# Two-block transformer step on one core: gate sums, turns, output norm and evictions moved in a hand-written order

## The chip, the cores and the metric

The kernel runs on one core of a Trainium2 chip, in one launch. The metric is device microseconds (us) of that core; lower is better. The engines are named as the profile names them: PE is TensorE, DVE is VectorE, ACT is ScalarE, POOL is GpSimd, SP is SyncE, which here only issues DMAs.

## The reference, cut to what matters

Two blocks follow each other on 256 latent tokens with 256 context tokens of width 1024, all in float32. The first block has two layers: a mixer out of a gated delta net and a chunked gated MLP, and multi-head latent attention (MLA); each has a gated feed-forward part with a depthwise convolution. The second block has dilated and sparse attention pairs (DIL, DSA), then cross attention (CRS) and an MLP. The change is mostly in the first mixer:

```python
def chunk_gmlp(u, v, ln_g, ln_b, ws, bs):                 # the "spatial" half, y_a
    u = gelu(u); v = layer_norm(gelu(v), ln_g, ln_b)
    s = einsum('gij,bnjgd->bnigd', ws, chunks(v)) + bs
    return u * s

def gdn_chunked(q, k, v, g, beta, s0):                    # the delta rule, y_b
    gcum = cumsum(g); decay = exp(tril(gcum_i - gcum_j))
    a_mat = strict_tril((k*beta) k^T * decay)
    t_mat = inverse(eye + a_mat)                          # built here in levels
    u = t_mat (v*beta);  w = t_mat (k*beta*exp(gcum))
    attn = q k^T * decay;  kdec = k * exp(gcum_end - gcum)
    scan over chunks: v_new = u - w s; o = (q*exp(gcum)) s + attn v_new
                      s = s * exp(gcum_end) + kdec^T v_new

def ab_mixer(...):
    a_u, a_v, qkv, gate, alpha, beta = split(h @ w_in)
    y_b = rms_norm(o_forward + o_backward, norm_g) * silu(gate)
    y = concatenate([y_a, y_b]) @ w_out                   # chunks 0-3 y_a, 4-7 y_b
```

Context tokens are scanned first (st=0), then the latent ones (st=1), which start from the context's final states.

## The kernel before, in words

**Projections.** Every weight is float32 and goes through the PE as a high and a low part in the rounded type fp32r. SP streams blocks of 512 KB into a ring of four slots. ACT's `split` (L1577) makes `w_high`, DVE's `low` (L2089) makes `w_low`, and `mm3` (L646 to L648) multiplies three times for each of the 8 chunks of 128: high by high, high by the low part of the activation, low by high. A tile is 128 output columns by up to 512 tokens, so 24 matmuls; tiles alternate between two banks, and ACT or DVE evicts each. For `low(t + 2)` to run, `split(t + 2)` must be done, and that waits for a PE tile that frees the slot.

**Order.** There is no planner. Each engine has its own hand-written instruction list, joined by semaphores, and each engine works strictly in the order of its list. Any instruction that waits holds everything that is behind it on its engine.

**The input projection, `in0`.** 25 tiles. The gates are tile 12 and are summed over tokens on the way: PE turns the gates and sums them (L792, L793) behind tile 16, out of `g_tok`, a copy by DVE (L2263). DVE makes cumulative sums and their combinations (L2265 to L2277), ACT takes one Exp of all of them (L1730), DVE multiplies two by beta (L2281, L2282; semaphore `g_fac`). Behind tile 18 PE spreads rows of these for the first quarter (L760, L761), and behind 20, 22 and 23 for the others (`ROWS_AT`). DVE also does `mod_tile(t)` in each tile (L2220, two products of 128x1024 for the modulation of a later layer), whose rows SP loads between the weight blocks.

**The levels.** 28 steps, 7 levels for 4 quarters, build the inverse. In each, PE multiplies (L893, L900), POOL masks (`lev_ct`, L1483), ACT evicts (`lev_m`, L1789), PE multiplies (L917, L920), DVE adds (L2385, L2386; in the first level L2359, L2380). Between the steps stand other jobs, given by the step number k: turns of the keys (L814, `TURNS`), spatial turns (L829), the layer norm of the spatial half on ACT, DVE and POOL (L1757, L1760, L2313 to L2321, L1507).

**The scan and `out0`.** Behind the scan of the latents come the output norm (ACT squares L1768, PE `out_sums` L850, ACT root L1772, DVE reciprocal L2333, PE `out_spread` L857, DVE L2341 and a product with the gate), then the split of y in high and low, then tiles 0 and 1 of `out0`, whose chunks 0 to 3 take y_a and 4 to 7 take y_b. The low parts of y_a are four DVE subtractions (L2432).

**Attention.** In `attend` (MLA, CRS) and `pair_step` (DIL, DSA) ACT takes the Exp of one step (L1941, L1960) and evicts the turned probabilities of the step before last, `probs_t` (L1947, L1967). PE turns probabilities (L1144, L1170) and multiplies by values (L1198, L1225, L1293). DVE does the maxima before the Exp and the divisions behind it.

## Time and profile before

| | us |
|---|---|
| median of 3 runs | 1676.14 |
| lowest, highest | 1676.03, 1677.31 |
| profiled execution, its own time | 1686.6 |
| its span, first to last instruction | 1684.8 |
| PE busy in it | 1568.6 (93%) |
| DVE, ACT, POOL busy | 1136.8, 797.0, 120.1 |
| mean granted PE clock | 0.965 |

Stages in the trace, us from the start of the span: `in0` ends about 219, levels of the context to about 278, scan of the latents to 391, `out0` from 398, MLA attention 922 to 972, DIL pairs 1309 to 1366, DSA pairs 1371 to 1402, CRS 1451 to 1469.

In a timeline row the first number is the start, the second the duration. A bracket at the end holds how long the engine had idled and which instruction released it. "x8" groups eight instructions, and the duration is that of the group from first start to last end.

### The profile page before, as it was taken

The page shows a single profiled execution, that of the slowest core. Times are in us where ns is not written, and L with a number is a line of the kernel's source. Part 1 is how long each engine was busy: PE and PEld are TensorE (multiplying, and loading weights), DVE is VectorE, ACT ScalarE, POOL GpSimd, SP SyncE. Part 2 cuts the span into 40 slices and gives each one's busy share as a digit, 9 for nine tenths or more (in the row PEclk, how much of TensorE's full clock was granted, in tenths as well). Part 3 has the DMA queues.
Part 4 walks back from the last instruction along what each step waited for, and adds up shares of the span by engine and source line. Part 5 has one row for each costly group of instructions (what it writes and reads, how often), then busy time and mean ns, then how long its engine had stood idle before and what let it go on. Part 6 is the DMA issues. An engine that isn't in the chain of part 4 may idle for free.

```text
span 1684.8 us, 30970 instructions
## 1 busy us (share of the span) xinstructions
PE 1568.6 (93%) x11414; PEld 1379.8 (82%) x11414; DVE 1136.8 (67%) x1902; ACT 797.0 (47%) x1436; POOL 120.1 (7%) x134
## 2 busy tenths in 40 slices
PE   5899978789999999999899999999999889999998
PEld 3687768788677777788787599999898668999998
DVE  5975765654599999966545458885565665477644
ACT  2553545142454444422255457775444445566532
POOL 2000032420100000000000010001000001010000
PEclk8999989999899999999899999999899999999999
DMA  9344420001155555555333035556443223255552
GB/s 356 118 176 161 150 77 3 2 3 38 63 188 186 187 182 179 182 180 174 122 125 100 2 101 187 187 187 214 160 163 126 88 75 104 98 188 184 178 195 91
DMA packets 62955, 230.77 MB, mean 137 GB/s; under 512 B 6800, under 2 KB 8080, under 8 KB 62352
## 3 DMA queue, kind: packets, MB, share of 16 engines
q1 hardware_dynamic: 61408, 223.37, 39.2%
q0 software_dynamic: 1168, 5.80, 1.0%
q8 instruction: 64, 1.05, 0.3%
q10 hardware_dynamic: 288, 0.33, 0.1%
q14 instruction: 27, 0.22, 0.0%
HBM read 228.43 MB, written 1.05 MB: 136 GB/s over the span
## 4 chain that ended last, share of the span: by engine, by line
PE 80%; DVE 11%; ACT 5%; issue 3%; POOL 1%; DMA 1%; DVEq 0%; ACTq 0%; POOLq 0%
PE proj L646 21%; PE proj L648 21%; PE proj L647 21%; DVE w_low L2089 2%; PE bank L698 1%; ACT w_high L1577 1%; PE bank L900 1%; PE bank L1198 1%; PE bank L917 1%; PE bank L920 1%; PE proj L1102 1%; PE proj L1103 1%; PE proj L1104 1%; DMA ident_sb<-ident 1%; DVE h_low L2122 1%
## 5 line engine op out<-in xcount | busy, mean ns | idle before, releaser
L646 PE MATMUL proj<-h_high,w_high 128*128 128x256 f32 (+1 forms) x1768 | 585.0, 331 | 22.3 <-DVE h_low L2122 13.7
L648 PE MATMUL proj<-h_high,w_low 128*128 128x256 f32 (+1 forms) x1768 | 571.6, 323 | 0.0
L647 PE MATMUL proj<-h_low,w_high 128*128 128x256 f32 (+1 forms) x1768 | 571.5, 323 | 0.0
L2089 DVE TENSOR_TENSOR w_low<-w_raw,w_high 128x1024 fp32r<-128x1024 f32 x322 | 393.3, 1224 | 191.0 <-ACT w_high L1577 189.6
L1577 ACT ACTIVATE w_high<-w_raw 128x1024 fp32r<-128x1024 f32 x322 | 338.5, 1056 | 243.8 <-PE proj L648 240.7
L646 PEld LDWEIGHTS proj<-h_high,w_high 128*128 128x128 f32 x1768 | 337.0, 191 | 65.0 <-issue 18.3
L648 PEld LDWEIGHTS proj<-h_high,w_low 128*128 128x128 f32 x1768 | 337.6, 191 | 27.6
L647 PEld LDWEIGHTS proj<-h_low,w_high 128*128 128x128 f32 x1768 | 337.1, 191 | 25.2
L648 PE MATMUL proj<-act_high,w_low 128*128 128x256 f32 (+1 forms) x608 | 189.9, 312 | 0.0
L646 PE MATMUL proj<-act_high,w_high 128*128 128x256 f32 (+1 forms) x608 | 189.5, 312 | 0.4 <-DVE w_low L2089 0.4
L647 PE MATMUL proj<-act_low,w_high 128*128 128x256 f32 (+1 forms) x608 | 189.5, 312 | 0.0
L646 PEld LDWEIGHTS proj<-act_high,w_high 128*128 128x128 f32 x608 | 114.1, 188 | 8.1 <-DVE w_low L2089 0.8
L647 PEld LDWEIGHTS proj<-act_low,w_high 128*128 128x128 f32 x608 | 113.8, 187 | 7.7
L648 PEld LDWEIGHTS proj<-act_high,w_low 128*128 128x128 f32 x608 | 114.3, 188 | 6.6
L1656 ACT ACTIVATE conv_in<-proj 128x512 f32<-128x512 f32 (+1 forms) x100 | 49.9, 499 | 120.3 <-PE proj L648 117.2
L2220 DVE SCALAR_TENSOR_TENSOR mod_products<-a_ring,cond_rows 128x1024 f32<-128x1024 f32 x80 | 103.6, 1295 | 0.1
L1450 POOL TENSOR_TENSOR tmp<-tmp 128x256 f32<-128x256 f32 (+1 forms) x40 | 43.7, 1099 | 797.5 <-ACT tmp L1593 619.0
L2220 DVE SCALAR_TENSOR_TENSOR a_ring<-a_ring,cond_rows 128x1024 f32<-128x1024 f32 x80 | 97.6, 1220 | 0.0
L2171 DVE SCALAR_TENSOR_TENSOR conv_mid<-conv_in,cols_sb,conv_mid 128x512 f32<-128x512 f32 (+1 forms) x100 | 63.5, 635 | 14.0 <-DVE conv_mid L2169 8.2
L2169 DVE SCALAR_TENSOR_TENSOR conv_mid<-conv_in,cols_sb,conv_mid 128x512 f32<-128x512 f32 (+1 forms) x100 | 63.3, 633 | 12.4 <-ACT conv_mid L1657 10.5
L1657 ACT ACTIVATE conv_mid<-proj,cols_sb 128x512 f32<-128x512 f32 (+1 forms) x100 | 58.9, 589 | 0.0
L2185 DVE SCALAR_TENSOR_TENSOR x<-proj,mod,x 128x256 f32 (+1 forms) x48 | 21.7, 480 | 48.1 <-PE proj L648 48.1
(406 smaller groups left out, 1917.7 us busy)
## 6 DMA issues: line engine op xcount, KB each, us to landing
w_raw<-w_stream SPq DMA_DIRECT2D x322, 512.0 KB, 3.3
a_ring<-a_stream SPq DMA_DIRECT2D x80, 512.0 KB, 3.2
a_first<-a_head SPq DMA_DIRECT2D x4, 1024.0 KB, 18.0
a_first<-a_stream SPq DMA_DIRECT2D x4, 1024.0 KB, 18.6
x<-x_in SPq DMA_DIRECT2D x1, 2048.0 KB, 10.4
late_tab<-late_tables POOLq DMA_DIRECT2D x1, 1408.0 KB, 6.5
cond_rows<-cond_rows SPq DMA_DIRECT2D x1, 1024.0 KB, 5.7
cond_rows<-cond_rows POOLq DMA_DIRECT2D x1, 1024.0 KB, 5.1
```

Source lines behind the costliest of these rows:

```text
L646: mm(out_, wh, xh, start=first, stop=False)
L647: mm(out_, wh, xl, start=False, stop=False)
L648: return mm(out_, wl, xh, start=False, stop=last)
L1450: nc.gpsimd.tensor_tensor(squares(name, 0), squares(name, 0), squares(name, k), ALU.add).then_inc(n_early, 1)
L1577: f(wh(n), RAW[:, n % 4, :], ACT.Copy).then_inc(w_high, 1)
L1656: f(XP[:, k % 2, 0:n, 1:SEQ + 1], PL[t % 2][:, 0:width].rearrange("p (s t) -> p s t", s=n), ACT.Copy)
L1657: f(C1[:, k % 2, 0:width], PL[t % 2][:, 0:width], ACT.Identity, scale=C[:, ds(taps + 3 * k + 1 + 3 * per * it, 1)]).then_inc(tile_out, 1)
L2089: v.tensor_tensor(wl(n), RAW[:, n % 4, :], wh(n), ALU.subtract).then_inc(w_low, 1)
L2169: v.scalar_tensor_tensor(o, XP[:, k % 2, 0:n, 0:SEQ], C[:, ds(taps + 3 * k + 3 * per * it, 1)], o, ALU.mult, ALU.add).then_inc(conv_mid, 1)
L2171: v.scalar_tensor_tensor(o, XP[:, k % 2, 0:n, 2:SEQ + 2], C[:, ds(taps + 3 * k + 2 + 3 * per * it, 1)], o, ALU.mult, ALU.add).then_inc(con ...
L2185: last = v.scalar_tensor_tensor(o, y, g, o, ALU.mult, ALU.add)
L2220: v.scalar_tensor_tensor(o, w, 1.0, cond[:, s, :], ALU.mult, ALU.mult, accum_out=MODF[:, ds(2 * (A_FIRST + j) + s + 2 * off, 1)]).then_inc ...
```

## The change

**A. `in0`.** DVE copies `g_tok` ahead of `low(18)` instead of behind it. The block of cumulative sums goes from tile 17 to the end of tile 16, the two products with beta from behind `low(20)` to ahead of it. ACT's Exp of the sums goes ahead of `split(19)`, with its wait. `mod_tile` gets ahead by one from tile 19 on, so that tile 23 has none. The closing of the modulation (L2096, L2102) and `low(26)` go into the levels, steps 3 and 6.

**B. Levels of the context.** The second turn of the keys is at step 8 instead of 6; the spatial turns, their evictions and each step of the layer norm are two or three steps later. POOL clears its 128x2048 table in two halves.

**C. Output.** The low parts of y_a are made on POOL. PE does tile 0's chunks 0 to 3 of `out0` ahead of `out_sums`, two chunks of tile 1 ahead of `out_spread` and two behind it, then the chunks of y_b for the context tokens, then for the latents. The products with the gate and the splits of the latents are in two halves.

**D. Evictions.** In `attend` and `pair_step` ACT evicts `probs_t` ahead of the Exp instead of behind it.

**E. `out2`.** 18 matmuls of tile 1 stand ahead of the last `dsa_out`.

```diff
-        TURNS = [(3, 6), (16, 20)]
+        TURNS = [(3, 8), (16, 20)]
 # PE, spatial_gate
-                if k in (9, 11):
+                if k in (12, 14):
 # PE, behind the scan
+            both = slice(0, T2)
+            weights(B0["out0"])
+            free_bank(T0["out0"])
+            pe.wait_ge(G["y_a"], 4)
+            out_part(0, range(4), both)
             out_sums(1)
+            weights(B0["out0"] + 1)
+            free_bank(T0["out0"] + 1)
+            out_part(1, range(2), both)
             out_spread(1)
-            first_tiles("out0", slice(0, T2), T2, lambda k: (G["y_a"], 4) if k < 4 else (G["y_b"], 2),
-                        [(j, k) for ks in (range(4), range(4, KC)) for j in range(2) for k in ks])
+            out_part(1, range(2, 4), both)
+            pe.wait_ge(G["y_b"], 1)
+            for j in range(2):
+                out_part(j, range(4, KC), CTX)
+            pe.wait_ge(G["y_b"], 2)
+            for j in range(2):
+                out_part(j, range(4, 6), LAT)
+            pe.wait_ge(G["y_b"], 3)
+            for j in range(2):
+                out_part(j, range(6, KC), LAT, KC - 1).then_inc(pe_done, 1)
 # PE, out2
+            out2_products(0)
             dsa_out(3)
-            project("out2", LAT, SEQ, lambda k: (A["at_y"], DSA.e0 + 2))
+            out2_products(1)
 # POOL, behind the levels of the latents
+            for d in range(2):
+                pool.wait_ge(sc_s[d], 3)
+            for t in range(4):
+                tok = slice(t * P, (t + 1) * P)
+                pool.wait_ge(G["sp_hi"], t + 1)
+                nc.gpsimd.tensor_tensor(HL[:, 0:4, tok], UV[:, 0:4, tok], HH[:, 0:4, tok], ALU.subtract).then_inc(G["y_a"], 1)
 # ACT, in0
             for t in range(GATES, 25):
+                if t == 17:
+                    act.wait_ge(G["g_cum"], 1)
+                    f(EX[:], EX[:], ACT.Exp).then_inc(G["g_exp"], 1)
                 if t < 24:
                     split(t + 2)
...
-                if t == 17:
-                    act.wait_ge(G["g_cum"], 1)
-                    f(EX[:], EX[:], ACT.Exp).then_inc(G["g_exp"], 1)
 # ACT, layer norm in the levels
-                if k in (10, 12):
+                if k in (13, 15):
-                if k in (14, 15):
+                if k in (17, 18):
-                if k == 16:
+                if k == 18:
                     act.wait_ge(G["ln_sq"], 4)
                     f(SM[:, 58:62], SM[:, 58:62], ACT.Sqrt, scale=1.0 / 512, bias=col("eps")).then_inc(G["ln_std"], 1)
-                if 18 <= k < 22:
+                if 20 <= k < 24:
 # ACT, attend (pair_step likewise)
+                    if 2 <= a < ly.n + 2:
+                        p = a - 2
...
+                        f(PT[:, p % 2, 0:ly.kt, :], ..., ACT.Copy).then_inc(A["at_pt"], 1)
                     if a < ly.n:
                         r = a % 3
                         act.wait_ge(A["at_m"], ly.a0 + a + 1)
...
-                    if 2 <= a < ly.n + 2:
-                        p = a - 2
...
 # DVE, in0
             for t in range(GATES, 24):
+                if t == 16:
+                    dve.wait_ge(G["g_tr"], 1)
+                    v.tensor_copy(GTOK[:], ...).then_inc(G["g_tok"], 1)
+                if t == 18:
+                    dve.wait_ge(G["g_exp"], 1)
+                    v.tensor_tensor(BE, BE, beta, ALU.mult)
+                    v.tensor_tensor(BR, BR, beta, ALU.mult).then_inc(G["g_fac"], 1)
                 low(t + 2)
...
+                if t in ROWS_AT:
+                    decays(0, ROWS_AT[t])
+                    triangles(0, ROWS_AT[t])
+                for j in ((t,) if t < 19 else (19, 20) if t == 19 else (t + 1,) if t < 23 else ()):
+                    mod_tile(j, CB0, PROD0)
...
+            def last_modulations(k):
+                if k == 3:
+                    dve.wait_ge(m_acc, 2 + 2 * MOD_IN)
+                    link(modulation(A_FIRST, MOD_IN))
+                    gains(0, 1).then_inc(mod_ready, 1)
+                if k == 6:
+                    low(26)
 # DVE, output norm
-                dve.wait_ge(G["on_n"], 2 * st + 2)
-                v.tensor_tensor(QKV[:, 8:12, x], QKV[:, 8:12, x], GATE[:, :, x], ALU.mult).then_inc(G["on_y"], 1)
+                for p in range(2):
+                    o = QKV[:, 8 + 2 * p:10 + 2 * p, x]
+                    dve.wait_ge(G["on_n"], 2 * st + p + 1)
+                    v.tensor_tensor(o, o, GATE[:, 2 * p:2 * p + 2, x], ALU.mult).then_inc(G["on_y"], 1)
```

DVE in `in0`, from tile 16 to tile 18. `w_low` is `low`, `g_cum` to `factors` the block of sums, and the `mod_products` and `a_ring` pair is one `mod_tile`. Before:

```order
106 L2089 TENSOR_TENSOR w_low<-w_raw,w_high 128x1024
107 L2268 TENSOR_SCALAR qk_log_factors<-qk_lengths 128x4x4
...
115 L2277 TENSOR_TENSOR factors<-qk_log_factors 128x32
116 L2220 SCALAR_TENSOR_TENSOR mod_products_100,mod<-a_ring,cond_rows_99 128x1024
117 L2220 SCALAR_TENSOR_TENSOR a_ring,mod<-a_ring,cond_rows_99 128x1024
118 L2089 TENSOR_TENSOR w_low<-w_raw,w_high 128x1024
119 L2281 TENSOR_TENSOR factors<-factors,g_tok 128x32
120 L2282 TENSOR_TENSOR factors<-factors,g_tok 128x32
```

The same place after:

```order
105 L2269 SCALAR_TENSOR_TENSOR a_ring,mod<-a_ring,cond_rows_99 128x1024
106 L2328 TENSOR_SCALAR qk_log_factors<-qk_lengths 128x4x4
...
114 L2337 TENSOR_TENSOR factors<-qk_log_factors 128x32
115 L2138 TENSOR_TENSOR w_low<-w_raw,w_high 128x1024
116 L2269 SCALAR_TENSOR_TENSOR mod_products_100,mod<-a_ring,cond_rows_99 128x1024
117 L2269 SCALAR_TENSOR_TENSOR a_ring,mod<-a_ring,cond_rows_99 128x1024
118 L2310 TENSOR_TENSOR factors<-factors,g_tok 128x32
119 L2311 TENSOR_TENSOR factors<-factors,g_tok 128x32
120 L2138 TENSOR_TENSOR w_low<-w_raw,w_high 128x1024
```

The sums have gone ahead of the `w_low` of tile 17, and the products with beta ahead of that of tile 18.

DVE where `in0` ends and the levels begin; `inv_u_halves` and `inv_t` are the first level's quarters. Before:

```order
154 L2248 TENSOR_TENSOR a_halves<-bank,decay 64x256 x2
155 L2251 TENSOR_TENSOR a_cross<-bank,decay 64x256
156 L2220 SCALAR_TENSOR_TENSOR mod_products_100,mod<-a_ring,cond_rows_99 128x1024
157 L2220 SCALAR_TENSOR_TENSOR a_ring,mod<-a_ring,cond_rows_99 128x1024
158 L2096 TENSOR_TENSOR mod<-mod,cols_sb 128x48
159 L2102 SCALAR_TENSOR_TENSOR gains<-mod,cols_sb 128x16
160 L2089 TENSOR_TENSOR w_low<-w_raw,w_high 128x1024
161 L2359 TENSOR_TENSOR inv_u_halves<-gdn_tab,lev_ct 128x256 x2
```

After:

```order
156 L2297 TENSOR_TENSOR a_halves<-bank,decay 64x256 x2
157 L2300 TENSOR_TENSOR a_cross<-bank,decay 64x256
158 L2414 TENSOR_TENSOR inv_u_halves<-gdn_tab,lev_ct 128x256 x2
159 L2435 TENSOR_TENSOR inv_t<-gdn_tab,bank 128x256 x2
160 L2414 TENSOR_TENSOR inv_u_halves<-gdn_tab,lev_ct 128x256
161 L2435 TENSOR_TENSOR inv_t<-gdn_tab,bank 128x256
162 L2414 TENSOR_TENSOR inv_u_halves<-gdn_tab,lev_ct 128x256
163 L2435 TENSOR_TENSOR inv_t<-gdn_tab,bank 128x256
164 L2145 TENSOR_TENSOR mod<-mod,cols_sb 128x48
```

The first level's products stand right behind `a_cross`; nothing of the modulation or of the next weight is between them.

PE where the scan of the latents ends and `out0` begins. Before:

```order
930 L970 MATMUL bank<-qkv,state 128x128 x4
931 L984 MATMUL bank<-attn_t,v_new 128x128 x8
932 L850 MATMUL bank<-ones,out_squares 128x1 x8
933 L857 MATMUL bank<-ident_sb,small 128x128 x8
934 L646 MATMUL proj<-h_high,w_high 128x512
935 L647 MATMUL proj<-h_low,w_high 128x512
```

After:

```order
931 L984 MATMUL bank<-attn_t,v_new 128x128 x8
932 L646 MATMUL proj<-h_high,w_high 128x512
...
943 L648 MATMUL proj<-h_high,w_low 128x512
944 L850 MATMUL bank<-ones,out_squares 128x1 x8
945 L646 MATMUL proj<-h_high,w_high 128x512
...
950 L648 MATMUL proj<-h_high,w_low 128x512
951 L857 MATMUL bank<-ident_sb,small 128x128 x8
952 L646 MATMUL proj<-h_high,w_high 128x512
```

Twelve matmuls of tile 0 now stand ahead of the sums of squares, and six of tile 1 between these and the spreading of the roots.

## Rows read from the trace of the kernel before

**Rows 1.** The page: busy us, share of the span and instructions of each engine.
```profile
PE 1568.6 (93%) x11414; PEld 1379.8 (82%) x11414; DVE 1136.8 (67%) x1902; ACT 797.0 (47%) x1436; POOL 120.1 (7%) x134
```

**Rows 2.** Waits of PE, 150 to 282 us: total, times, longest.
```profile
PE bank L893 <- POOL lev_ct L1483: 4.3, 1, 4.3
...
PE proj L814 <- DVE k_decay L2302: 2.6, 1, 2.6
PE proj L829 <- DVE k_decay L2302: 2.6, 1, 2.6
```

**Rows 3.** Timeline of PE around the gate sums and the first spread rows.
```profile
155.66 0.40 PE L648 MATMUL proj<-h_high,w_low 128*128 128x512 f32 x1
158.75 0.40 PE L792 MATMUL bank<-g_tok,gdn_tab 128*128 128x16 f32 x2 [2.70 <-DVE g_tok L2263]
...
160.09 0.77 PE L646 MATMUL proj<-h_high,w_high 128*128 128x512 f32 x1
...
173.48 0.39 PE L647 MATMUL proj<-h_low,w_high 128*128 128x512 f32 x1
173.71 0.40 PE L648 MATMUL proj<-h_high,w_low 128*128 128x512 f32 x1
176.77 0.80 PE L760 MATMUL bank<-ident_sb,log_rows 128*128 128x128 f32 x2 [2.67 <-DVE factors L2282]
...
179.96 0.48 PE L646 MATMUL proj<-h_high,w_high 128*128 128x512 f32 x1
```

**Rows 4.** Windows: us, busy (count) of PE, PEld, DVE, ACT, POOL; clock, DMA.
```profile
160.00:166.00 6.00, 6.00 (x16) 4.74 (x16) 0.99 (x2) 0.00 (x0) 0.00 (x0) 0.50 0.49 175
...
176.00:180.00 4.00, 3.23 (x17) 3.23 (x17) 0.71 (x3) 2.44 (x3) 0.00 (x0) 0.57 0.63 237
...
225.00:231.00 6.00, 6.00 (x88) 5.55 (x86) 1.96 (x4) 1.36 (x6) 2.95 (x5) 0.51 0.40 146
...
244.00:248.00 4.00, 4.00 (x69) 3.80 (x69) 0.44 (x2) 1.54 (x5) 0.73 (x1) 0.57 0.02 4
...
391.00:399.00 8.00, 5.91 (x35) 5.73 (x36) 3.26 (x7) 1.33 (x2) 0.00 (x0) 0.79 0.01 2
```

**Rows 5.** Timeline of DVE at tile 16.
```profile
157.24 1.23 DVE L2089 TENSOR_TENSOR w_low<-w_raw,w_high 128x1024 fp32r<-128x1024 f32 x1 [2.56 <-ACT w_high L1577]
158.38 0.32 DVE L2263 COPY g_tok<-bank 128x160 f32<-128x160 f32 x1
```

**Rows 6.** Timeline of DVE at the start of the levels.
```profile
218.88 1.74 DVE L2220 SCALAR_TENSOR_TENSOR mod_products<-a_ring,cond_rows 128x1024 f32<-128x1024 f32 x1
...
223.28 0.75 DVE L2359 TENSOR_TENSOR inv_u_halves<-gdn_tab,lev_ct 128x256 f32<-128x256 f32 x2
```

**Rows 7.** Timeline of ACT in the layer norm: table load and root.
```profile
259.66 1.28 ACT L1760 ACT_TABLE_LOAD   x1
260.96 0.30 ACT L1760 ACTIVATE small<-small,cols_sb 128x4 f32<-128x4 f32 x1
```

**Rows 8.** Timeline of PE behind the scan of the latents.
```profile
392.50 1.95 PE L850 MATMUL bank<-ones,out_squares 128*128 128x1 f32 x16 [1.93 <-ACT out_squares L1768]
395.04 3.52 PE L857 MATMUL bank<-ident_sb,small 128*128 128x128 f32 x16 [0.60 <-DVE small L2333]
```

**Rows 9.** Timeline of POOL in the layer norm.
```profile
266.11 1.28 POOL L1507 TENSOR_TENSOR uv<-uv,ln_rows_sb 128x512 f32<-128x512 f32 x1 [0.69 <-DVE uv L2321]
```

**Rows 10.** Timelines of ACT and of PE in MLA.
```profile
934.61 0.59 ACT L1947 ACTIVATE probs_t<-bank 128x512 f32<-128x512 f32 x1
...
934.54 0.66 PE L1144 MATMUL bank<-ident_sb,probs 128*128 128x128 f32 x4
935.25 1.16 PE L1198 MATMUL bank<-probs_t,mla_v 128*128 128x128 f32 x8
```

**Rows 11.** Waits of PE on evicted probabilities, in DIL and in DSA.
```profile
PE bank L1225 <- ACT probs_t L1967: 1.7, 3, 0.6
PE bank L1293 <- ACT probs_t L1967: 2.2, 4, 0.7
```

More of the change, by code:

```diff
@@ L819, in spatial_gate @@
             def spatial_gate(k):
-                if k in (9, 11):
-                    for t in (k - 9, k - 8):
+                if k in (12, 14):
+                    for t in (k - 12, k - 11):
                         if t >= 2:
@@ L985, in _, with out_part @@
                         last.then_inc(sc_o[d], 1)
+            def out_part(j, chunks, x, final=None):
+                n, t = B0["out0"] + j, T0["out0"] + j
+                for k in chunks:
+                    w = slice(k * P, (k + 1) * P)
+                    last = mm3(PL[t % 2][:, x], wh(n)[:, w], wl(n)[:, w], HH[:, k, x], HL[:, k, x], k == 0, k == final)
+                return last
+            both = slice(0, T2)
[3 more added lines that the diff above has]
+            out_part(0, range(4), both)
             out_sums(1)
+            weights(B0["out0"] + 1)
+            free_bank(T0["out0"] + 1)
+            out_part(1, range(2), both)
             out_spread(1)
-            first_tiles("out0", slice(0, T2), T2, lambda k: (G["y_a"], 4) if k < 4 else (G["y_b"], 2),
-                        [(j, k) for ks in (range(4), range(4, KC)) for j in range(2) for k in ks])
+            out_part(1, range(2, 4), both)
[8 more added lines that the diff above has]
+                out_part(j, range(6, KC), LAT, KC - 1).then_inc(pe_done, 1)
             for s in (2, 3):
@@ L1307, in _, with out2_products @@
                     dsa_out((a - 6) // 2)
-            dsa_out(3)
-            project("out2", LAT, SEQ, lambda k: (A["at_y"], DSA.e0 + 2))
+            out2_order = [(1, k) for k in (4, 5, 6, 7, 0, 2)], [(0, k) for k in (4, 5, 6, 7, 0, 2, 1, 3)] + [(1, 1), (1, 3)]
+            def out2_products(part):
+                n, t = B0["out2"], T0["out2"]
+                for i, (j, k) in enumerate(out2_order[part]):
+                    if i == 0:
+                        weights(n + j)
+                        free_bank(t + j)
+                        pe.wait_ge(A["at_y"], DSA.e0 + 1 + part)
+                    w = slice(k * P, (k + 1) * P)
+                    last = mm3(PL[(t + j) % 2][:, 0:SEQ], wh(n + j)[:, w], wl(n + j)[:, w], HH[:, k, LAT], HL[:, k, LAT], k == 4, k == 3)
+                    if k == 3:
+                        last.then_inc(pe_done, 1)
+            out2_products(0)
+            dsa_out(3)
+            out2_products(1)
+            for s in (2, 3):
+                tile(B0["out2"] + s, T0["out2"] + s, LAT, SEQ)
+            with pe.Fori(1, 2) as i:
+                for s in range(4):
+                    tile(B0["out2"] + s, T0["out2"] + s, LAT, SEQ, 4 * i)
             project("xq", CTX, SEQ, h_ready("cross"), beside="cross")
@@ L1953, in pair_step @@
             def pair_step(ly, a, out_bank, out_chunk):
+                if 2 <= a < ly.n + 2:
+                    p = a - 2
+                    nk = 1 + p % 2
+                    act.wait_ge(A["at_t"], ly.a0 + p + 1)
+                    act.wait_ge(A["at_o"], ly.a0 + p - 1)
+                    f(PT[:, p % 2, 0:2 * nk, :], BK[2 + p % 2][:, 0:2 * nk * P].rearrange("p (k q) -> p k q", k=2 * nk), ACT.Copy).then_inc(A["at_pt"], 1)
                 if a < ly.n:
@@ L2277, in _ @@
                     v.tensor_tensor(BR, by_k, by_q, ALU.subtract).then_inc(G["g_cum"], 1)
-                if t == 18:
-                    beta = GTOK[:, :, 32:40].rearrange("p t (d h) -> p t d h", d=2)
-                    dve.wait_ge(G["g_exp"], 1)
-                    v.tensor_tensor(BE, BE, beta, ALU.mult)
-                    v.tensor_tensor(BR, BR, beta, ALU.mult).then_inc(G["g_fac"], 1)
-                    dve.wait_ge(gdn_in, 16)
-                if t in ROWS_AT:
-                    decays(0, ROWS_AT[t])
-                    triangles(0, ROWS_AT[t])
-                mod_tile(t, CB0, PROD0)
-            dve.wait_ge(m_acc, 2 + 2 * MOD_IN)
-            link(modulation(A_FIRST, MOD_IN))
-            gains(0, 1).then_inc(mod_ready, 1)
-            low(26)
+            def last_modulations(k):
+                if k == 3:
+                    dve.wait_ge(m_acc, 2 + 2 * MOD_IN)
[3 more added lines that the diff above has]
+                    low(26)
             def keys(st, k):
@@ L2427, in _ @@
                         ins.then_inc(sc_out[d], 1)
+            dve.wait_ge(G["on_hi"], 1)
+            v.tensor_tensor(HL[:, 4:8, CTX], QKV[:, 8:12, CTX], HH[:, 4:8, CTX], ALU.subtract).then_inc(G["y_b"], 1)
             out_factor(1)
[L2429 to L2432 removed]
             out_norm(1)
[L2434 to L2436 removed]
+            for p in range(2):
+                dve.wait_ge(G["on_hi"], 2 + p)
+                v.tensor_tensor(HL[:, 4 + 2 * p:6 + 2 * p, LAT], QKV[:, 8 + 2 * p:10 + 2 * p, LAT], HH[:, 4 + 2 * p:6 + 2 * p, LAT], ALU.subtract).then_inc(G["y_b"], 1)
             def project(name, width=None, gate=None, loops=2):
```

57 lines of the change are left out of this document (24 added, 33 removed).

## The prediction, as it was put on record before the changed kernel ran

> **What bounds the kernel now.** I read the page first: PE is busy for 93% of the span, DVE for 67%, ACT for 47% [rows 1]. The change removes no matmul, so it can gain only where PE stands idle, and where PE runs at half its clock. Next I read PE's waits by stage. In the 130 us around the end of `in0` and the levels there are a few long ones: 4.3 us on POOL's mask, and two of 2.6 us on DVE's `k_decay` [rows 2]; two of 2.7 us stand at the gate sums [rows 3]. Third, the windows: behind each of these waits the granted clock is 0.50 to 0.57 for some us, though PE is busy all through [rows 4]. So such a wait costs twice: its own time, and the lost clock behind it (a granted 0.50 is 1.2 GHz, 1.00 is 2.4 GHz). Last I read what DVE and ACT do just before PE is released.
>
> The sum is made against the profiled execution (1686.6 us), which is 10.5 us above the median of 1676.14. These savings are microseconds of waits, so I take them off the median unscaled.
>
> **Part A, gate sums, -10.5 us.** Tile 16 of PE ends at 155.7+0.4, and DVE copies `g_tok` at 158.38 only because `low(18)` stands before it, and waits 2.56 us for ACT and then takes 1.23 [rows 5]. The copy needs nothing of ACT's. Moved ahead, it is done before PE gets there: PE's 2.70 goes. From the last product of tile 16 to tile 17 are 4.43 us (155.66 to 160.09); one product pace of 0.23 and the four small products at full clock, about 0.9, remain, so 3.3 are saved. Then the clock: from 160 to 166 it was 0.50 [rows 4], so that from the first to the last product of tiles 17 and 18, 160.09 to 173.71, it took 13.6 us; 47 products, 0.23 apart as at 173.48 and 173.71 [rows 3], are 10.7: 2.9 saved. The second wait, 2.67 at 176.77, ends with `factors` L2282 [rows 3]: this now stands ahead of `low(20)`, and the sums ahead of `low(19)`. By durations of before, the sums are done at about 161.8, the Exp at 162.4, the two products at 167.4 behind `low(19)` and `mod_tile`, and tile 18 ends at 167.8: in time by 0.4. From 173.71 to 179.96 are 6.25 us, of which one product's pace and the sixteen small ones at full clock (0.11 each, as the levels' pace of 0.106 shows) need 1.9: 4.3 saved. 3.3 + 2.9 + 4.3 = 10.5.
> What is late next? ACT's Exp now holds `split(19)`. That one is released by the end of tile 17, at 162.3, so it is late by some 0.1 us, and its cover is tile 18 (5.5 us) before its high part is needed. `mod_tile` one ahead: DVE may wait 0.2 to 0.5 us for a row that SP loads; the cover is the same tile. If the clock does not recover, only the two waits go: -5.4, the small end. There is no large end beyond 10.5, since PE then runs with no gap.
>
> **Part B, start of the levels and turns, -12.2 us.** PE waits 4.3 us for the first level's masks, since POOL waits for DVE. DVE comes to the first level's products at 223.28, after 4.4 us of modulation, gains and `low(26)` that begin at 218.88 [rows 6]. These now stand in steps 3 and 6. The wait of 4.3 [rows 2] goes, and with it the six us at 0.51, which are 2.9 of lost clock (6 x 0.49) [rows 4]; 0.5 stays, for the masks of POOL which each follow PE's product by a short wait. 4.3 + 2.9 - 0.5 = 6.7. Behind that, the key turn's 2.6 goes: a step of the levels is about 1.4 us, so step 8 instead of 6 gives DVE 2.8 us more to make `k_decay`. Of the spatial turn's 2.6 I leave 1.2, since it is three steps later, but the key turn ahead of it has moved by two and `low(26)` (1.22 us) is now in between: 1.4 saved, and 1.5 of the four us at 0.57 [rows 2, 4]. 6.7 + 2.6 + 1.4 + 1.5 = 12.2. The layer norm keeps its length: each job moves by two or three steps. The root now falls in the same step as the last squares, so its table load may hold an eviction of the levels by 1.3; the next steps, which have nothing else on ACT, give it back. Small end: only the first 4.3 and the key turn, -6.9. Large end -14, if the spatial wait goes altogether.
> The row for the table load shows 1.28 us, and the root starts 0.02 us behind its end [rows 7]; ACT's eviction before it had ended at the load's start. The Trainium skill, page "ScalarE: Activation LUTs", section "What ACT_TABLE_LOAD costs", gives about 1283 ns and a drain of about 1380 ns for each switch. The load agrees; the drain is not in this trace. By the page the root in step 18 would cost an estimated 1.4 us more, and part B would be 10.8.
>
> **Part C, output, -4.2 us.** PE idled 1.93 for ACT's squares and 0.60 for the root, and the 16 spread products took 3.52 us [rows 8] where 1.8 is full clock: the window shows 0.79 [rows 4]. Now twelve products (2.7 us) fill the first wait and six (1.4) the second; 1.93 + 0.60 + 1.7 = 4.2. They need the low parts of y_a before about 390.4, where the scan ends. POOL makes four of 128x512; a POOL product of that size took 1.28 [rows 9], so 5.1 us, from about 384.1, when the third state is out: done at 389.2. Bound: 1.76 each, as POOL's sums of squares go (L1450), ends at 391.1, and PE waits 0.7. The four DVE subtractions that went away hid behind the spread and gain nothing by themselves. Small end -2.5, large end -5.
>
> **Part D, evictions first, -6.1 us.** In MLA the turn that began at 934.54 is four products and over by 935.0, but the values' products behind it began at 935.25, when the eviction of 934.61, which stood behind an Exp, had ended (935.20) [rows 10]. That is 0.2 in a period of 6.2 us, which repeats some seven times: -1.5. In DIL the wait on `probs_t` is 1.7 in three places [rows 11]; it goes, and one copy's length more, 0.6 to 0.7, comes off the wait for the divisions behind it: -2.4. In DSA the four waits sum to 2.2 [rows 11], all on the copy that stood behind two Exps: -2.2. The cost is an Exp that starts one copy later, 0.59; it is hidden while the Exp waits for DVE's maximum. Ends: -3 if the waits just go over to the divisions, -9 if the clock too is held in DIL.
>
> **Part E, `out2`, 0.** Eighteen half-width products of 0.12 us are 2.1 us, moved ahead of the last `dsa_out`; PE then waits for the same split of the last chunk. From -1.5 to +0.7.
>
> Sum: -10.5 - 12.2 - 4.2 - 6.1 = -33.0. One us back for new short dips of the clock: -32, so 1676.1 - 32 = 1644.1.
>
> **The rivals.** *R1, the waits move within the levels.* DVE and ACT have the same work in fewer us, and the turns, which wait for DVE's products, come as late as before against the start of the levels. For it: both turns wait for the same DVE line [rows 2]. Against it: the moves are 2.8 and 4.2 us of steps against waits of 2.6. Then B gives only 4: -24, 1652. *R2, the clock stays low.* The waits go, but the granted clock falls elsewhere in these stages, since many waits of 0.3 to 0.7 remain. It costs back 2.9 + 1.6 (A), 2.9 + 1.5 (B) and 1.7 (C), together 10.6, less the 1 allowed: -22.4, 1654. *R3, more than the sum.* The large ends of B, C and D: -42, 1634. *R4, slower.* One mechanism: evicting first puts the Exp behind a copy that waits for PE's turns, and the new wait of ACT before `split(19)` does the same in `in0`; PE gets more short waits in place of a few long ones, and is granted half the clock over long stretches. For it: two stages got more waits of ACT on PE. Place: levels, scan and attention, where most windows show 0.95 to 1.00. Half the clock costs one us for each us of products, so it turns slower when more than 33 us of PE's work go at 0.5 that now go at 1.0; for 50 us it gives +17, 1693. Against it: the low stretches of these stages all stand behind waits of 1.9 us or more [rows 2, 3, 8]. *R5, nothing moves.* If the new gate wait on ACT held as long as the old ones on DVE, A is nothing; all parts would have to fail: 1676. The order of instructions shows each move, so this is small.
>
> **How the numbers follow.** Forecast (-26 to -39) 0.70; R1 0.12; R2 0.08; R3 0.05; R4 0.02; R5 0.03. The small ends together (5.4 + 6.9 + 2.5 + 3 - 0.7) are -17.1, or 1659; the large ends, taken as not all coming together, -40, or 1636. The range 1636 to 1658 holds the forecast, R1 and R2 and most of the unknown costs, and leaves out R3 to R5. A measurement of this kernel can tell 0.2%, 3.4 us, from no change. Faster 0.95, same 0.03, slower 0.02.
>
> **What would show it.** Right: no idle of PE before `g_tok` and `factors`, clock near 1.00 from 155 to 180; the first level starts within 1 us of the end of `in0`; PE goes from the scan into `out0` with no gap; waits on `probs_t` gone in DSA. Wrong: PE waits at the spread of tile 18 on `factors` (A's margin is 0.4 us), at the turns on `k_decay`, at L893 on POOL, at tile 0 of `out0` on POOL's subtraction; or the same waits gone, but windows at 0.5 beside them.

## The result, and the profile after

| | before | after |
|---|---|---|
| median of 5 runs, us | 1676.6 | 1652.93 |
| lowest, highest | 1676.03, 1679.1 | 1649.54, 1654.63 |
| ratio, 95% interval | | 0.9846 [0.9831, 0.986] |
| profiled execution, its span | 1684.8 | 1647.8 |
| mean granted PE clock in it | 0.965 | 0.977 |

The medians differ by 23.7 us; the two traced executions by 37.0. A second measurement of both kernels (below) gave 0.9818 [0.9795, 0.984], -30.6 us. Both intervals lie wholly below 1, so the changed kernel is faster, by 1.5 to 1.8%. The forecast was -32. Some microseconds stand between these numbers, and they are the subject of the first experiment.

The page of the changed kernel, engines and granted clock:

```profile
PE 1546.7 (94%) x11438; PEld 1364.2 (83%) x11438; DVE 1133.9 (69%) x1901; ACT 796.8 (48%) x1437; POOL 124.6 (8%) x139
...
PEclk9999999999899999999899999999899999999999
```

PE has 22 us less busy time than in [rows 1], though it does the same products: what went there is PE at half its clock. (Against a second trace of the kernel before, below, it is 13 us.) The matmul count differs by missing records and by the split tiles.

**Gate sums.** The timeline of ACT and that of DVE, changed kernel, around tiles 17 and 18:

```profile
161.00 0.31 ACT L1766 ACTIVATE factors<-factors 128x128 f32<-128x128 f32 x1 [2.94 <-DVE factors L2337]
161.63 1.06 ACT L1625 ACTIVATE w_high<-w_raw 128x1024 fp32r<-128x1024 f32 x1 [0.32 <-PE proj L648]
```

```profile
166.26 0.19 DVE L2311 TENSOR_TENSOR factors<-factors,g_tok 128x32 f32<-128x32 f32 x1
```

ACT's Exp is over at 161.31 and `split(19)` still idles 0.32 us for PE behind it, so the new wait ahead of it costs nothing. The second product with beta ends at 166.45; PE uses it at 166.87, a margin of 0.4 us. PE shows no idle time where [rows 3] had 2.70 and 2.67. The windows of the changed kernel (us, busy and count of PE, PEld, DVE, ACT, POOL, clock, DMA) show the full clock through `in0` and the levels, where [rows 4] had 0.50, 0.57 and 0.51:

```profile
155.00:165.00 10.00, 10.00 (x49) 8.38 (x48) 6.86 (x16) 6.08 (x7) 0.00 (x0) 1.00 0.58 208
165.00:175.00 10.00, 10.00 (x53) 8.51 (x52) 7.38 (x19) 4.53 (x6) 1.29 (x1) 1.00 0.29 106
...
207.00:213.00 6.00, 4.84 (x106) 4.02 (x106) 5.59 (x12) 2.01 (x4) 4.45 (x7) 1.00 0.01 3
```

**Levels.** PE's waits, 200 to 262 us, changed kernel:

```profile
PE bank L917 <- ACT lev_m L1837: 3.9, 3, 1.8
PE proj L829 <- DVE k_decay L2355: 1.2, 1, 1.2
...
PE bank L893 <- POOL lev_ct L1523: 0.5, 1, 0.5
```

Against [rows 2] the first masks cost 0.5 in place of 4.3, the key turn nothing in place of 2.6, the spatial turn 1.2 in place of 2.6. The waits on ACT's evictions grew: L917 from 2.6 in four to 3.9 in three, and L924 from 0.6 in two to 1.2 in three.

**Output.** The timeline of PE behind the scan, changed kernel:

```profile
370.15 1.84 PE L850 MATMUL bank<-ones,out_squares 128*128 128x1 f32 x16
373.34 1.95 PE L857 MATMUL bank<-ident_sb,small 128*128 128x128 f32 x16
...
384.11 0.50 PE L646 MATMUL proj<-h_high,w_high 128*128 128x512 f32 x1 [1.78 <-DVE w_low L2138]
```

Both waits of [rows 8] are gone, and the spread takes 1.95 us in place of 3.52. But a wait that nobody had before stands ahead of tile 2: 1.78 us.

### The profile page after: what moved, and what is told of

It reads as the page before. It is cut to its first block, busy times and chain, and to the rows that moved or that the text cites. A ratio compares the mean times of both kernels' runs of the same rounds, so it can differ in the third digit from the quotient of the medians.

```text
span 1647.8 us, 31024 instructions
## 1 busy us (share of the span) xinstructions
PE 1546.7 (94%) x11438; PEld 1364.2 (83%) x11438; DVE 1133.9 (69%) x1901; ACT 796.8 (48%) x1437; POOL 124.6 (8%) x139
## 3 DMA queue, kind: packets, MB, share of 16 engines
q8 instruction: 64, 1.05, 0.3%
HBM read 228.43 MB, written 1.05 MB: 139 GB/s over the span
## 4 chain that ended last, share of the span: by engine, by line
PE 80%; DVE 11%; ACT 4%; issue 3%; POOL 1%; DMA 1%; DVEq 0%; ACTq 0%; POOLq 0%
PE proj L646 22%; PE proj L648 21%; PE proj L647 21%; DVE w_low L2138 2%; PE bank L698 1%; PE bank L900 1%; ACT w_high L1625 1%; PE bank L920 1%; PE bank L917 1%; DVE conv_mid L2218 1%; DMA ident_sb<-ident 1%; PE proj L1122 1%; DVE h_low L2171 1%; DVE tmp L2182 1%; PE bank L706 1%
## 6 DMA issues: line engine op xcount, KB each, us to landing
x<-x_in SPq DMA_DIRECT2D x1, 2048.0 KB, 10.5
```

## The experiments

All ratios are against the kernel before, in the same call. "Gate tile" is the time from ACT's `w_high` number 19 to number 21 (`split(18)` to `split(20)`), "tile 18" from there to number 23. "The levels" is the time from PE's first L893 to its first L949. A window is given as us, busy and count of PE, PEld, DVE, ACT, POOL, clock, DMA.

### The kernel before, traced again

> The kernel before, unchanged, for a second trace of it. Theory 1 (the low clock behind each long wait belongs to the kernel): the windows 160:166, 176:180, 225:231, 244:248 and 391:399 show 0.5 to 0.8 again, and the trace is again some 10 us longer than the median of the plain runs. Theory 2 (the first trace was an unlucky execution): the trace is within 3 us of 1676.5, and 7 to 10 us of lost clock at those windows or elsewhere are missing from it.

No edit. 1677.78 us, 10 runs from 1675.82 to 1686.29; ratio 1.0006 [0.9988, 1.0023]. Its traced execution has a span of 1674.5, 10.3 less than the first. Timeline of PE, kernel before, second trace, then its windows, each at the same distance from the wait as in [rows 4]:

```profile
157.01 0.40 PE L792 MATMUL bank<-g_tok,gdn_tab 128*128 128x16 f32 x2 [2.70 <-DVE g_tok L2263]
173.43 0.49 PE L760 MATMUL bank<-ident_sb,log_rows 128*128 128x128 f32 x2 [2.67 <-DVE factors L2282]
```

```profile
158.25:164.25 6.00, 6.00 (x21) 4.79 (x20) 0.99 (x2) 0.00 (x0) 0.00 (x0) 0.72 0.48 175
172.65:176.65 4.00, 3.22 (x22) 3.00 (x23) 1.77 (x7) 2.45 (x3) 0.00 (x0) 1.00 0.64 231
220.30:226.30 6.00, 5.98 (x121) 5.47 (x119) 2.27 (x5) 1.95 (x8) 3.16 (x5) 0.73 0.39 150
239.30:243.30 4.00, 3.80 (x60) 3.67 (x62) 0.05 (x1) 1.54 (x5) 0.73 (x1) 0.66 0.01 4
386.95:394.95 8.00, 5.89 (x35) 5.72 (x36) 3.25 (x7) 1.32 (x2) 0.00 (x0) 0.79 0.01 2
```

The waits are the same to 0.01 us: 2.70 and 2.67. The clock behind them is not: 0.72 where it had been 0.50, 1.00 where it had been 0.57, 0.73 where it had been 0.51. The last two windows are nearly as before (0.66 and 0.79, against 0.57 and 0.79). Two executions of each kernel, put side by side by the starts of ACT's `w_high`; stretches that show little or no difference are left out, the longest of them, from behind MLA to `dn1`, with 289.73, 288.07, 288.74 and 289.04 us:

| stretch, us | before | before, again | after | after, again |
|---|---|---|---|---|
| start | 46.74 | 45.02 | 45.70 | 46.30 |
| gate tile | 18.05 | 16.45 | 11.91 | 11.91 |
| tile 18 | 17.09 | 15.73 | 12.79 | 12.79 |
| levels, scans, to `out0` tile 0 | 187.83 | 188.53 | 174.02 | 173.80 |
| `out0` tiles 0 to 2 | 13.94 | 13.74 | 13.93 | 15.33 |
| up to and with MLA | 556.81 | 556.21 | 554.89 | 555.00 |
| `dn1` to `in2` | 27.11 | 23.96 | 23.97 | 23.97 |
| DIL | 64.35 | 64.28 | 62.06 | 62.05 |
| DSA and `out2` | 55.18 | 54.37 | 52.45 | 52.46 |
| CRS | 36.73 | 36.72 | 36.16 | 36.12 |

The first trace held 1.6 + 1.4 us of lost clock more at the gate sums than the second, 3.2 more in `dn1` (which the change does not touch), and 1.7 each in the start and in the stretch behind MLA. So theory 2 holds for the time and for the gate sums: that execution had lost more clock than most. It does not hold for the levels and the scan, which took 188.53 us in the second trace against 187.83: there the clock that the forecast counts on was lost in both, partly in other places. All runs of the kernel before taken together (62) have a median of 1678.1, and 21 of them are above 1680; the changed kernel's ten lie between 1649.5 and 1654.6.

### Part A alone

```diff
+                if t == 17:                       # ACT, ahead of split(19)
+                    f(EX[:], EX[:], ACT.Exp).then_inc(G["g_exp"], 1)
...
+                if t == 16:                       # DVE, ahead of low(18)
+                    dve.wait_ge(G["g_tr"], 1)
+                    v.tensor_copy(GTOK[:], ...).then_inc(G["g_tok"], 1)
...
+                mod_tile(t, CB0, PROD0)          # as before, for its own tile
```

> The kernel before with part A's moves alone (copy of g_tok, sums, Exp and the products with beta moved ahead; the modulation rows stay with their tiles). Theory 1: -10.5 us, 1666. Theory 2 (waits only, the clock behind them is mostly not lost in a usual execution): -5.4 to -7, 1670.

1671.3 us; 0.9971 [0.9957, 0.9986], -4.9 (the two medians differ by 6.5). The gate tile and tile 18 take 11.9 and 12.8 us in its trace, as in the changed kernel. Against the second trace of before that is -7.5, against the first -10.4. The ratio's interval, -7.2 to -2.3, takes in -7 and leaves out -10.5, so it speaks for theory 2; its middle is below both. The two tiles themselves take 24.7 us in every one of the eight traces with the whole of part A, and 32.2 to 35.1 in the five that have none of it.

### Part B alone

```diff
-        TURNS = [(3, 6), (16, 20)]
+        TURNS = [(3, 8), (16, 20)]
...
+                        last_modulations(k)       # steps 3 and 6 of the levels
```

> The kernel before with part B alone: turns, layer norm, POOL's clearing and the closing of the modulation and low(26) moved, modulation rows one tile ahead. Theory 1: -12.2 us, 1664. Theory 2: waits only, -8, 1668.

1668.05 us; 0.9941 [0.9927, 0.9955], -9.9 [-12.2, -7.6], which does not tell the two theories apart. The trace does more. From the first L893 to the first L949 its trace takes 47.35 us (216.88 to 264.23), before's two took 58.39 and 58.97. So -11.0 to -11.6 in the levels, of the 12.2. It repeats: the five traces without part B have 58.3 to 59.1 us here, the seven with part B as it is 47.1 to 48.1. Windows over exactly this stretch, kernel before (second trace), then changed kernel:

```profile
214.54:273.51 58.97, 45.06 (x1121) 42.24 (x1121) 34.30 (x74) 26.46 (x71) 25.05 (x31) 0.89 0.13 47
```

```profile
207.88:255.82 47.94, 40.09 (x1120) 37.50 (x1120) 31.67 (x70) 26.37 (x71) 24.69 (x32) 1.00 0.12 36
```

PE has 13.9 us without work before and 7.9 after, so about 6 of the 11 us are waits. The other 5 are much the same products (1121 and 1120 records) at a higher clock.

### Part C alone

```diff
+            out_part(0, range(4), both)
             out_sums(1)
...
+            out_part(1, range(2), both)
             out_spread(1)
...
```

> The kernel before with part C alone: the low parts of y_a on POOL, and out0's products among the sums and the spreading of the output norm. The forecast was -4.2 us. The trace of the changed kernel says less: a new wait of 1.78 us for a weight's low part stands behind tiles 0 and 1, so -2.4 with the clock's 1.7 and -1 without.

1678.16 us; 1.0007 [0.9997, 1.0018]: nothing. Its trace, PE's timeline and a window:

```profile
405.79 0.50 PE L646 MATMUL proj<-h_high,w_high 128*128 128x512 f32 x1 [1.78 <-DVE w_low L2116]
```

```profile
406.00:411.00 5.00, 5.00 (x16) 3.93 (x16) 1.66 (x3) 0.70 (x2) 1.52 (x1) 0.66 0.55 210
```

From the first L949 of the latents to tile 2 it gains 2.3 us (37.53 against 39.8 in the second trace of before). Behind the new wait the clock is 0.66 for five us, which takes 1.6 back (15.33 us for `out0` tiles 0 to 2, against 13.74). Six traces have this wait, each with 1.78 us. In three of them (this one, the second of the changed kernel, and the kernel with the closing put back) the five us behind it are at 0.66, in the other three at 1.00.

### Part D alone

```diff
+                if 2 <= a < ly.n + 2:             # ACT: probs_t first
+                    f(PT[...], BK[2 + p % 2]..., ACT.Copy).then_inc(A["at_pt"], 1)
                 if a < ly.n:                      # then the Exp
```

> The kernel before with part D alone, the evictions of the turned probabilities ahead of the Exp in all four attention stages. The forecast said -6.1: -1.5 in MLA, -2.4 in DIL, -2.2 in DSA. The two traces so far put -2.1, -2.2, -1.9 and -0.6 (CRS) there, -6.8 with out2's part. Rival (the waits go over to the divisions): -3 or less. 1671.

1671.99 us; 0.9947 [0.9928, 0.9965], -8.9 [-12.1, -5.9]. PE's waits in DIL, kernel before (second trace), then part D alone:

```profile
PE bank L1170 <- DVE probs L2596: 5.9, 6, 1.7
PE bank L1225 <- ACT probs_t L1967: 1.7, 3, 0.6
```

```profile
PE bank L1170 <- DVE probs L2596: 6.6, 6, 1.8
```

The waits on `probs_t` are gone, and 0.7 of their 1.7 went over to the divisions (0.4 against the first trace, which has 6.2 there), where the forecast had expected 0.6 to 0.7 to come off as well. So PE waits 1.0 to 1.3 less in DIL, but the stage is 2.2 shorter, in each of the traces with part D (62.0 to 62.1 us, against 64.3 to 64.4). The rest is in no wait of PE; the granted clock of the stage went from 0.95 to 0.97. How the two share it is not shown. In DSA, changed kernel, 0.2 is left of [rows 11]'s 2.2:

```profile
PE bank L1190 <- DVE probs L2650: 3.6, 4, 1.4
...
PE bank L1313 <- ACT probs_t L2008: 0.2, 1, 0.2
```

By the table the stages give -2.2 (DIL), -1.9 (DSA with `out2`) and -0.6 (CRS), and the stretch up to and with MLA -1.2 to -1.3, together -6.0. Two of these hold more than part D. The stretch up to MLA is mostly projections. MLA's attention by itself, from ACT's first Exp there to `w_high` number 121, takes 52.9 us in four traces without part D (both of before, parts A and C alone) and 50.9 to 51.0 in four with it (part D alone, both of the changed kernel, without part E): -2.0. And DSA with `out2` takes 51.62 us with part D alone, against 54.37: -2.7; in the changed kernel part E takes 0.8 of that back (below). So part D gives -2.0, -2.2, -2.7 and -0.6, -7.5 in all. The rival (-3 or less) is refuted.

### The changed kernel again

> The changed kernel, unchanged, for a second trace on another day of the chip and a second ratio. If its granted clock is 1.00 through part A's and B's stretches again (150 to 262 us), the clock there belongs to the kernel without long waits; if dips come back, it is drawn anew in each execution. Time: 1651 to 1654.

No edit. 1650.05 us; 0.9818 [0.9795, 0.984], -30.6. Windows of its trace:

```profile
146.00:166.00 20.00, 20.00 (x95) 16.33 (x94) 13.16 (x28) 7.62 (x9) 0.00 (x0) 1.00 0.49 182
...
214.00:256.00 42.00, 35.20 (x1012) 33.38 (x1009) 26.89 (x60) 24.61 (x68) 20.66 (x26) 1.00 0.13 41
256.00:267.00 11.00, 10.31 (x78) 10.12 (x77) 3.20 (x5) 3.72 (x9) 0.00 (x0) 0.85 0.01 1
```

From 146 to 256 us the clock is 1.00 again. Behind the levels the first trace had 1.00 and this one 0.85. That the clock stays up in the levels is not certain in each execution, though: a kernel below whose levels are the same (tile 0 of `out0` finished first) has no wait over 1.8 us there and shows

```profile
242.00:247.00 5.00, 4.43 (x98) 4.43 (x100) 1.22 (x5) 2.33 (x6) 0.74 (x1) 0.66 0.01 3
```

Over the whole execution the lost clock (the span times what the mean granted clock lacks to 1) was about 60 and 48 us in the two traces of the kernel before, and 38 and 40 in those of the changed kernel. So the change gave back 8 to 9 us of it against the second trace of before, and 20 to 21 against the first.

### One wait put back

```diff
-                if t == 16:
-                    dve.wait_ge(G["g_tr"], 1)
-                    v.tensor_copy(GTOK[:], ...).then_inc(G["g_tok"], 1)
...
                 low(t + 2)
+                if t == 16:
+                    dve.wait_ge(G["g_tr"], 1)
+                    v.tensor_copy(GTOK[:], ...).then_inc(G["g_tok"], 1)
```

> The changed kernel with one wait put back: DVE copies g_tok behind low(18). PE waits 2.7 us again. Theory 1 of the forecast (a wait of this size always takes the clock with it): 160:166 shows 0.5 and the gate tile takes 18.0 us in place of 11.9. Theory 2 (how far the clock falls is drawn anew in each execution): the wait is 2.70 to 0.02, and the gate tile takes anything from 15 to 18; median +3.5 to +5.

1656.8 us; 0.9872 [0.9849, 0.9896]: +5.6 against the median of all ten of the changed kernel (1651.2), +4 against the kernels without part C and without part E, timed beside it. The trace:

```profile
158.30 0.39 PE L792 MATMUL bank<-g_tok,gdn_tab 128*128 128x16 f32 x2 [2.70 <-DVE g_tok L2313]
```

```profile
157.00:163.00 6.00, 4.70 (x19) 3.96 (x20) 4.59 (x15) 1.83 (x3) 0.00 (x0) 0.77 0.46 157
```

The wait is 2.70 to the hundredth. The gate tile takes 16.43 us, +4.5. Over the six traces that have this wait (before twice, parts B, C and D alone, and this one) it took 18.05, 16.45, 18.03, 16.63, 16.44 and 16.43. From the last product of tile 16 to the first of tile 17 PE takes 4.01 us here, and 1.05 in the changed kernel: so the wait costs 3.0, and the clock behind it 1.6 to 1.8 in four executions and 3.2 in two. The mean granted clock of the gate tile is 0.90 in the four and 0.81 in the two. The forecast was read from one of the two. Its split, 3.3 for the wait and 2.9 for the clock, puts 0.4 of the clock into the wait, since in that trace the four small products already ran slowly (4.43 us for the same way).

### The closing of the modulation put back

```diff
-                for j in ((t,) if t < 19 else (19, 20) if t == 19 else (t + 1,) if t < 23 else ()):
-                    mod_tile(j, CB0, PROD0)
+                mod_tile(t, CB0, PROD0)
...
+            dve.wait_ge(m_acc, 2 + 2 * MOD_IN)
+            link(modulation(A_FIRST, MOD_IN))
+            gains(0, 1).then_inc(mod_ready, 1)
+            low(26)
```

> The changed kernel with the modulation rows back at their own tiles, and the closing of the modulation and low(26) back at the end of in0. The forecast's step: PE's wait of 4.3 us for the first masks comes back, with up to 2.9 us of clock behind it: +4 to +7. Rival (the waits only move within the levels, since the turns are late against their start): +2 or less.

1658.49 us; 0.988 [0.9858, 0.9903]: +6.0 against the kernel without part C, timed beside it, and +7.3 against the median of all ten of the changed kernel (1651.2). PE's timeline, then a window:

```profile
213.42 1.97 PE L893 MATMUL bank<-ident_sb,lev_ct 64*64 64x64 f32 x32 [4.27 <-POOL lev_ct L1523]
```

```profile
214.00:220.00 6.00, 6.00 (x108) 5.54 (x106) 1.72 (x4) 1.61 (x7) 2.92 (x5) 0.62 0.33 127
```

The levels take 53.94 us (208.01 to 261.95) against 47.94 and 47.13. The forecast's term was 6.7. The rival (+2 or less) is refuted.

### Without part C

```diff
-            out_part(0, range(4), both)
             out_sums(1)
-            out_part(1, range(2), both)
             out_spread(1)
...
+            first_tiles("out0", slice(0, T2), T2, ...)
```

> The changed kernel without part C: the output norm and out0's first tiles in the order of before. Theory 1 (C saves 2.3 us at tile 2's start and sometimes loses 1.6 of it to the clock behind its new wait): +1 to +2.5 us against the changed kernel's 1650 to 1653. Rival (what C alone showed, no gain): 0.

1652.52 us; 0.9847 [0.9821, 0.9873]. The two stretches of the table that end with tile 2 of `out0` take 190.69 us, against 187.95 and 189.13 with part C in the changed kernel's traces, and 189.23 and 189.46 in the two kernels with part C that were timed beside it. So C gives 1.2 to 2.7, and the clock, in the levels as behind its own wait, makes up the difference. The medians (1650.1 to 1652.9 with it) cannot tell that from nothing.

### Without part E

```diff
-            out2_products(0)
             dsa_out(3)
-            out2_products(1)
+            project("out2", LAT, SEQ, lambda k: (A["at_y"], DSA.e0 + 2))
```

> The changed kernel without part E: out2's products all behind the last output chunk, as before. Forecast: 0, from -0.7 to +1.5; the wait of 1.5 us for the last chunk's low part is there with both.

1652.98 us; 0.9843 [0.9817, 0.9869]. PE's timeline in `out2`, changed kernel, then without part E:

```profile
1366.64 1.08 PE L1321 MATMUL proj<-o_lat,w_uv_sb 128*64 128x256 f32 x4
1369.22 0.36 PE L646 MATMUL proj<-h_high,w_high 128*128 128x256 f32 x1 [1.50 <-DVE h_low L2654]
```

```profile
1365.66 1.83 PE L1321 MATMUL proj<-o_lat,w_uv_sb 128*64 128x256 f32 x8
1369.00 0.36 PE L646 MATMUL proj<-h_high,w_high 128*128 128x256 f32 x1 [1.50 <-DVE h_low L2634]
```

The same wait stands in both, 1.50 us, and the medians cannot tell the kernels apart (1650.1 to 1652.9 with part E). But the traces can. DSA with `out2` takes 51.61 us here and 51.62 with part D alone, against 52.45 and 52.46 in the changed kernel; the next stretch gives 0.2 of it back. So part E costs 0.6 us in these traces. With it the last four products of `dsa_out` (L1321) stand behind the eighteen, so the last chunk's split starts later by as much, and PE waits its 1.50 all the same. That lies inside the forecast's ends (-1.5 to +0.7), and the moved products bought nothing.

### Tile 0 of `out0` finished first

```diff
             pe.wait_ge(G["y_b"], 1)
-            for j in range(2):
-                out_part(j, range(4, KC), CTX)
+            out_part(0, range(4, KC), CTX)
+            out_part(1, range(4, 6), CTX)
...
+            out_part(0, range(6, KC), LAT, KC - 1).then_inc(pe_done, 1)
+            out_part(1, range(6, KC), CTX)
+            out_part(1, range(4, KC), LAT, KC - 1).then_inc(pe_done, 1)
```

> The changed kernel with another order of the last products of out0's tiles 0 and 1: tile 0's latent chunks as soon as they are there, and half of tile 1's context chunks behind them. Theory (part C's new wait of 1.78 us on a weight's low part exists because both tiles end together and so free their weight slot late): the wait falls to about 0.6 and tile 2 begins 1.2 to 1.3 us earlier, -1.2 against the changed kernel, more where the clock fell behind the wait. Rival (the slot was not what held it): no change, or +0.7 for a wait on the latents' low part.

1649.26 us; 0.9806 [0.9781, 0.983], against 0.9818 of the changed kernel in the same call. PE's waits, 364 to 390 us, changed kernel, then this one:

```profile
PE proj L646 <- DVE w_low L2138: 1.8, 1, 1.8
```

```profile
PE proj L646 <- DVE w_low L2138: 0.4, 1, 0.4
```

The wait came from tiles 0 and 1 ending together: ACT's next `w_high` was released by tile 0's end. From the spread (L857) to the norm's first sum (L698) it takes 42.70 us, against 44.46 and 45.44, and 43.85 to 45.45 in the other kernels with all of part C's order: 1.2 to 2.8 less, of which 1.4 is the wait and the rest the clock. That the whole kernel is faster than the changed one is not shown: -0.8 in medians, and each ratio is uncertain by 4 us either way. The trace's stretch is what speaks for it.

### Squares of the layer norm spread over four steps

```diff
-                if k in (17, 18):
+                if 17 <= k < 21:
                     act.wait_ge(G["ln_mean"], 1)
-                    for t in (2 * k - 34, 2 * k - 33):
+                    for t in (k - 17,):
...
-                if k == 18:
+                if k == 20:
```

> The same, and in the context's levels one square of the layer norm in each of steps 17 to 20 in place of two in 17 and 18, the root in step 20, and the later steps two further. Theory (the waits of 1.46, 1.82 and 0.61 us on ACT's eviction in the changed kernel's levels come from two squares of 0.9 us and a table load of 1.28 us that stand ahead of it): the first goes, the second stays: -1.5 to -2 against the run before it. Rival (the norm then ends late behind the levels): the same time is lost at the spatial products, 0.

1650.82 us; 0.982 [0.9797, 0.9842]. It also has the order of the run before. PE's waits on ACT in its levels:

```profile
PE bank L924 <- ACT lev_m L1837: 2.7, 3, 1.1
PE bank L917 <- ACT lev_m L1837: 1.4, 3, 0.6
```

L917 fell from 3.9 to 1.4 and L924 rose from 1.2 to 2.7. The levels take 46.75 us, against 47.94 and 47.13: at most -1.2, and nothing in the median. Of 5.1 us of these waits 4.1 are left, so they moved more than they went; ACT has the same work in these steps. The expected gain of 1.5 to 2 us is not there.

## Why the prediction held, and where it did not

**A, gate sums, forecast -10.5.** The mechanism held, and its margin to the tenth: the copy, the sums, the Exp over at 161.31 (forecast 162.4), `factors` with 0.4 us to spare (forecast 0.4). All of it comes about 1 us earlier than forecast, as the start of this trace is 1 us shorter. Against the first trace the stretch is 10.4 shorter. Against the second it is 7.5, and part A alone measured -4.9 [-7.2, -2.3]. The term that was mis-sized is the clock: the forecast took 2.9 + 1.6 from windows of one execution, which had lost more there than most. The second, 1.6 at the spread rows, was not lost at all in three of five traces (15.73).

**B, levels, forecast -12.2.** Alone -9.9; in the levels' own stretch -10.2 to -12.0 over all traces. The start of the levels was worth 6 to 7 (forecast 6.7), the key turn's wait went, 1.2 of the spatial turn's stayed, as said. What the forecast had wrong is that the layer norm keeps its length and that the steps behind the root give its time back: waits on ACT's evictions rose from 3.2 to 5.1 (L917 and L924 together), where two squares and the table load stand in one step. That these cause it is shown in part only: spreading the squares took 1.0 of the 5.1 away. The drain that the Trainium skill gives for a table load ("ScalarE: Activation LUTs", "What ACT_TABLE_LOAD costs") was not seen: the load in the changed kernel begins at 241.32, 0.02 us behind the last square, and ends at 242.60, and the root starts at 242.61.

```profile
241.32 1.28 ACT L1808 ACT_TABLE_LOAD   x1
242.61 0.30 ACT L1808 ACTIVATE small<-small,cols_sb 128x4 f32<-128x4 f32 x1
```

**C, output, forecast -4.2.** -1.2 to -2.7 by traces, nothing that a median tells. Both waits and the spread's clock came back as forecast (4.1 us). The step that failed is what is not in it: "what is late next" was asked of POOL's subtractions, which were in time (the last over at 365.5, while PE still had the scan's last products, from 365.59), and not of the weight slot. The new order ends tile 0 and tile 1 together; `split` waits for tile 0; that costs 1.78, and in half of the traces 1.4 to 1.6 of clock behind it.

**D, evictions, forecast -6.1.** -7.5 in traces, -8.9 [-12.1, -5.9] alone. MLA gave 2.0 for 1.5, DSA 2.7 for 2.2, and CRS, counted at nothing, 0.6. In DIL the 2.2 are near the forecast's 2.4 by luck: its second half, a shorter wait on the divisions, did not come, that wait grew.

**E, forecast 0.** +0.6 by traces.

**The sum.** The largest mis-sized term belongs to the base: "These savings are microseconds of waits, so I take them off the median unscaled". The waits are; the clock terms, 10.6 us in all, were read from an execution that was itself 10.5 above the median, and 3 us of that distance were clock terms of part A. Next comes C's new wait, 2. With the second trace's figures the sum is -7.5 (A), -11.4 (B), -2.2 (C), -7.5 (D), +0.6 (E), together -28.0, and the measured ratios say -25.8 and -30.6. Part of the nearness to -32 is luck: D's surplus of 1.4 covers most of what C lacks. The parts measured alone add to -22.5 (-4.9, -9.9, +1.2, -8.9); with some 2.5 us of uncertainty in each, it stays open whether the parts together give more than their sum.

**The rivals.** The first measurement, 1652.9 us, lies at the times of R1 (1652) and R2 (1654) and just outside the band of the forecast itself (-26 to -39), with -25.8 by the ratio and -23.7 by the medians; the second, -30.6, lies inside. So the time alone decides nothing between these three; the traces do. R1 (waits move within the levels, B gives only 4) is refuted by the levels' stretch, 10.2 to 12.0 shorter, and by the kernel with the closing put back. R2 (the clock falls elsewhere and costs 10.6 back) is refuted by both traces of the changed kernel, which lost 8 to 9 us less of clock than the second of before, and 20 to 21 less than the first. R3 to R5 are refuted by the time. (R3's -42 was too large by its own terms: the large ends of B, C and D add to -38.5.)

## What to carry to other kernels

Price a wait at its own length first, which repeats to 0.01 us, and the clock behind it as a range from several executions; one trace that is 10 us above the median is a poor source for it. When filler work is put between the last steps of a tile, look at what the end of that tile releases: two tiles that end together free their weight slots late, and a new wait takes the place of the old. When work is moved ahead of an engine's last step, look at whether the wait behind that step moves with it: then the move gains nothing and delays the step. A copy that needs nothing belongs ahead of the instruction that waits, on an engine that keeps the order of its list.

## What the runs showed of the hardware

The same idle time of PE (2.70 us, releaser and length equal) was followed by 1.6 to 1.8 us of lost clock in four executions and by 3.2 in two; the granted clock of the gate tile was 0.90 in the four and 0.81 in the two. In the changed kernel, where from 146 to 256 us no idle time of over 2 us is left, the granted clock there was 1.00 in both traces; in the kernel that finishes tile 0 first, with the same levels, it was 0.66 from 242 to 247. A wait of 1.78 us was followed by 1.00 in three traces and by 0.66 in three. Executions of the kernel before ranged over 12 us (1674.8 to 1686.6), those of the changed kernel over 5. A table load of 1.28 us on ACT had 0.02 us ahead of it and 0.01 behind it.
